# Splitting the first two weight tiles of a convolved projection, and multiplying half of the first, inside the projection before it

## The reference, cut to what matters

```python
h = rmsnorm(x, norm_g[l, 0]) * (1.0 + sc1) + sh1
z = h @ mix_in
za = dwconv3(z[..., :IN_COLS_A], mix_conv)
r, k, v, u = jnp.split(za, 4, -1)
qb, kb, vb = (t.reshape(B_, S_, N_HEADS_B, HEAD_DIM) for t in jnp.split(z[..., IN_COLS_A:], 3, -1))
```

## Time and profile before

| | us |
|---|---|
| median of 3 runs | 2668.36 |
| lowest and highest run | 2662.7 and 2673.42 |
| the profiled execution, its own time | 2661.84 |
| its span, first to last instruction | 2659.8 |
| TensorE busy in the span | 2489.5 (94%) |
| VectorE, ScalarE, GpSimd busy | 1674.4, 1158.0, 1063.9 |
| mean granted TensorE clock | 0.973 |

### The profile page before, as it was taken

One profiled execution on the slowest core, in us unless ns is written; L12 is line 12 of the kernel. 1 busy time (PEld: TensorE's weight loads), 2 busy tenths in 40 slices (PEclk: granted clock), 3 DMA queues, 4 the chain that ended last, 5 costly groups with the idle time before them and its releaser, 6 DMA issues. The chain is left out here.

```text
span 2659.8 us, 51660 instructions
## 1 busy us (share of the span) xinstructions
PE 2489.5 (94%) x21215; PEld 2005.1 (75%) x21215; DVE 1674.4 (63%) x2450; ACT 1158.0 (44%) x1886; POOL 1063.9 (40%) x717
## 2 busy tenths in 40 slices
PE   6998999798999989899999999987989999999998
PEld 5776666577888877778888878765777888887876
DVE  7775632474666546666565676856566666667686
ACT  5211343564555533444444444454444444444453
POOL 0301122202222202258888843331325787884333
PEclk9999999898999999999999999997999999999999
DMA  7776544803222124224343355231222434335423
GB/s 248 238 263 221 176 153 189 243 18 81 75 75 75 51 90 135 90 73 127 115 127 103 119 202 159 66 119 72 88 95 68 127 115 127 103 119 205 155 72 127
DMA packets 301965, 339.45 MB, mean 128 GB/s; under 512 B 29056, under 2 KB 207989, under 8 KB 301733
## 3 DMA queue, kind: packets, MB, share of 16 engines
q1 hardware_dynamic: 292092, 329.83, 38.4%
q10 hardware_dynamic: 9640, 6.33, 0.8%
HBM read 253.23 MB, written 82.88 MB: 126 GB/s over the span
## 5 line engine op out<-in xcount | busy, mean ns | idle before, releaser
L3410 POOL TENSOR_TENSOR first_over_u_lo<-first_over_u_raw,first_over_u_hi 128x512 fp32r<-128x512 f32 x210 | 319.5, 1529 | 120.2 <-ACT first_over_u_hi L3237 120.2
L3237 ACT ACTIVATE first_over_u_hi<-first_over_u_raw 128x512 fp32r<-128x512 f32 x210 | 128.6, 630 | 378.3 <-POOL first_over_u_raw L3428 147.5
L136 PE MATMUL cg_ps<-m_hi,first_over_u_hi 128*128 128x512 f32 x544 | 211.6, 389 | 0.0
L137 PE MATMUL cg_ps<-m_lo,first_over_u_hi 128*128 128x512 f32 x544 | 211.6, 389 | 0.0
L138 PE MATMUL cg_ps<-m_hi,first_over_u_lo 128*128 128x512 f32 x544 | 211.6, 389 | 0.0
L3486 DVE SCALAR_TENSOR_TENSOR cg_z<-cg_ps,top_conv_f,cg_z 128x1023 f32<-128x1023 f32 x84 | 107.8, 1283 | 73.9 <-ACT cg_z L3262 73.9
L136 PE MATMUL first_over_ps<-over_y_tx,first_over_u_hi 128*128 128x512 f32 x320 | 124.5, 389 | 0.0
L137 PE MATMUL first_over_ps<-over_y_tx,first_over_u_hi 128*128 128x512 f32 x320 | 124.5, 389 | 0.0
L138 PE MATMUL first_over_ps<-over_y_tx,first_over_u_lo 128*128 128x512 f32 x320 | 124.5, 389 | 0.0
L3410 POOL TENSOR_TENSOR first_over_u_lo<-cg_u_s,first_over_u_hi 128x512 fp32r<-128x512 f32 x80 | 103.4, 1292 | 50.5 <-ACT first_over_u_hi L3237 50.5
L138 PEld LDWEIGHTS cg_ps<-m_hi,first_over_u_lo 128*128 128x128 f32 x544 | 102.1, 188 | 21.4
(11 more groups left out here) (553 smaller groups left out, 7186.1 us busy)
## 6 DMA issues: line engine op xcount, KB each, us to landing
first_over_u_raw<-in_ffn_up SPq DMA_DIRECT2D x88, 512.0 KB, 5.0
qkv_mw<-in_ada_w SPq DMA_DIRECT2D x12, 2048.0 KB
scr_act<-cg_z SPq DMA_DIRECT2D x44, 512.0 KB, 2.6
raw_over_h_b<-in_ffn_down SPq DMA_DIRECT2D x56, 256.0 KB, 3.0
first_over_u_raw<-scr_act SPq DMA_DIRECT2D x44, 256.0 KB, 4.5
first_over_u_raw<-scr_asum SPq DMA_DIRECT2D x44, 256.0 KB, 2.6
scr_asum<-cg_over_split_sums SPq DMA_DIRECT2D x42, 256.0 KB
qkv_mw<-in_ada_w SPq DMA_DIRECT2D x8, 1024.0 KB, 11.5
```

The costliest lines, as they stand in the source:

```text
L136: nc.tensor.matmul(out, a_hi, b_hi, start=first, stop=False)
L137: nc.tensor.matmul(out, a_hi, b_lo, start=False, stop=False)
L3237: A(u_hi[:, n % RING], source(g, i), ACT.Copy).then_inc(uhi_done, 1)
L3410: G.tensor_tensor(u_lo[:, n % RING], source(g, i), u_hi[:, n % RING].bitcast(F32), ALU.subtract).then_inc(ulo_done, 1)
```

## The change

A class `FirstTiles` holds the raw, high and low parts of the first two weight tiles and the PSUM tile of the convolved projection, at addresses that are valid in both functions (its `ps` lies on the banks of `qkv_ps`; the high and low parts lie on the half of `qkv_w_hi` that column block 1 used). The splits of tiles 0 and 1 by ScalarE move into steps 20 and 21 of the q, k, v projection, after the copies that ScalarE makes there, and the two subtractions by GpSimd follow them. TensorE makes tile 0's product over the first 512 tokens in the function before: four of the eight k ahead of the last `add_up` (chunk 11), four behind it. The convolved projection then starts with `second_half(0)`.

```diff
--- before.py
+++ after.py
@@ -143,7 +143,29 @@
     t for f in range(WA // P) for t in (f, 2 * (WA // P) + f)]
 
 
-def features_and_qkv(nc, x_src, cond, mix_in, columns, x, xt, h_hi, h_lo, consts, rope_cos, rope_sin, qk_d, v_d, ada_w, ada_b, mod_d):
+class FirstTiles:
+
+    def __init__(self, nc, s, h_hi, h_lo):
+        self.nc, self.h_hi, self.h_lo = nc, h_hi, h_lo
+        self.raw = s.sb("raw", [P, 2, KT, P])
+        s.sb("x", [P, WA // P, S])
+        self.hi, self.lo = s.sb("w_hi", [P, 2, KT, P], F32R), s.sb("w_lo", [P, 2, KT, P], F32R)
+        self.ps = s.ps("ps", [P, 2, S])
+        self.hi_done, self.lo_done = s.sem("hi_done"), s.sem("lo_done")
+
+    def split(self, act, j):
+        self.nc.scalar.activation(self.hi[:, j], self.raw[:, j], ACT.Copy).then_inc(self.hi_done, 1)
+
+    def low(self, pool, j):
+        pool.wait_ge(self.hi_done, j + 1)
+        self.nc.gpsimd.tensor_tensor(self.lo[:, j], self.raw[:, j], self.hi[:, j].bitcast(F32), ALU.subtract).then_inc(self.lo_done, 1)
+
+    def products(self, k):
+        split_products(self.nc, self.ps[:, 0, 0:HALF], self.hi[:, 0, k, :], self.lo[:, 0, k, :], self.h_hi[:, k, 0:HALF], self.h_lo[:, k, 0:HALF],
+                       k == 0, k == KT - 1)
+
+
+def features_and_qkv(nc, x_src, cond, mix_in, columns, x, xt, h_hi, h_lo, consts, rope_cos, rope_sin, qk_d, v_d, ada_w, ada_b, mod_d, tiles):
 
 
 
@@ -156,8 +178,7 @@
     with ExitStack() as ctx:
         s = Scope(nc, ctx, "qkv")
         R = 4
-        with ExitStack() as octx:
-            w_next = Scope(nc, octx, "next").sb("w", [P, 2, KT, P])
+        w_next = tiles.raw
         w_raw = s.sb("w_raw", [P, R, WA])
         w_hi = s.sb("w_hi", [P, 2, KT, WA], F32R)
         w_lo = s.sb("w_lo", [P, 2, KT, WA], F32R)
@@ -341,6 +362,10 @@
                     for c in range(CM):
                         if summed_at(c) == cb * TT + t:
                             chunk_out(c)
+                    if cb == NC - 1 and t in (4, 5):
+                        act.wait_ge(next_loaded, 32)
+                        act.wait_ge(mm_done, TT * cb)
+                        tiles.split(act, t - 4)
                 if cb + 2 < NC:
                     split(cb + 2)
             for j in range(2):
@@ -360,6 +385,8 @@
                 pool.wait_ge(hi_done, n + 1)
                 nc.gpsimd.tensor_tensor(w_lo[:, cb % 2, k, :], w_raw[:, n % R, :], w_hi[:, cb % 2, k, :].bitcast(F32),
                                         ALU.subtract).then_inc(lo_done, 1)
+            tiles.low(pool, 0)
+            tiles.low(pool, 1)
 
         @block.vector
         def _(dve):
@@ -542,11 +569,17 @@
                         turn(n - 1)
                     for c in range(CM):
                         if summed_at(c) == n:
+                            if c == CM - 1:
+                                pe.wait_ge(tiles.lo_done, 1)
+                                pe.wait_ge(staged, n - 1)
+                                for k in range(KT // 2):
+                                    tiles.products(k)
                             pe.wait_ge(ms.acc_done, c + 1)
                             if c >= 2:
                                 pe.wait_ge(ms.row_done, c - 1)
                             ms.add_up(c % 2, c % 2)
-    return w_next
+            for k in range(KT // 2, KT):
+                tiles.products(k)
 
 
 CH = 64
...
@@ -580,8 +613,10 @@
     with ExitStack() as ctx:
         s = Scope(nc, ctx, "za")
         s.sb("w_place", [P, 2, KT, P])
-        w_hi, w_lo = s.sb("w_hi", [P, 2, KT, P], F32R), s.sb("w_lo", [P, 2, KT, P], F32R)
-        u, kt = s.sb("u", [P, KU, S]), s.sb("k", [P, KU, S])
+        u = s.sb("u", [P, KU, S])
+        s.sb("w_hi_place", [P, 2, KT, P]), s.sb("w_lo_place", [P, 2, KT, P])
+        w_raw, w_hi, w_lo, hi_done, lo_done = tiles.raw, tiles.hi, tiles.lo, tiles.hi_done, tiles.lo_done
+        kt = s.sb("k", [P, KU, S])
         rt, vt, both = (s.sb(n, [P, 2, S]) for n in ("r", "v", "both"))
         kk = u
         lw = s.sb("lw", [P, 3, KU, P])
@@ -590,14 +625,15 @@
         out = s.sb("out", [P, 4, S])
         pick, spread = s.sb("pick", [P, 32]), s.sb("spread", [P, P])
         rest, eps = s.sb("rest", [P, KU]), s.sb("eps", [P, 1])
-        ps, pr = s.ps("ps", [P, 2, S]), s.ps("pr", [P, 2, S])
+        s.ps("ps_place", [P, 2, S])
+        ps, pr = tiles.ps, s.ps("pr", [P, 2, S])
...
@@ -846,7 +882,8 @@
                 pe.wait_ge(bonus_in, f + 1)
                 product(f"H{f}", heads[:, :], both[:, f % 2, :], result(f"H{f}"))
 
-            for p in range(3):
+            second_half(0)
+            for p in range(1, 3):
                 tile(p)
             chunk_sum(0)
             tile(3)
@@ -912,10 +949,8 @@
             A = nc.scalar.activation
 
             def split(p):
-                if p >= 2:
-                    act.wait_ge(raw_loaded[p % 2], 16 * (p // 2))
-                if p >= 2:
-                    act.wait_ge(mm_done, p - 1)
+                act.wait_ge(raw_loaded[p % 2], 16 * (p // 2))
+                act.wait_ge(mm_done, p - 1)
                 A(w_hi[:, p % 2], w_raw[:, p % 2], ACT.Copy).then_inc(hi_done, 1)
 
             def middle(p):
@@ -987,8 +1022,6 @@
                 act.dma_start(mod_d[1, (E0 + c) * CHUNK:(E0 + c + 1) * CHUNK].rearrange("(o n) -> o n", o=1),
                               in_slot(bon, c)[0:1, :]).then_inc(m_stored[c % 2], 16)
 
-            split(0)
-            split(1)
             for p in range(3):
                 step(p)
             chunk_out(0)
@@ -1072,7 +1105,7 @@
                 pool.wait_ge(rated, f + 1)
                 G.tensor_tensor(both[:, f % 2, :], both[:, f % 2, :], kt[:, f, :], ALU.mult).then_inc(rated_k, 1)
 
-            for p in range(11):
+            for p in range(2, 11):
                 low(p)
             sum_rates(0)
             low(11)
...
```

More of the change, by code:

```diff
@@ L560, in project_and_prepare @@
 def project_and_prepare(nc, mix_in, conv_cols, h_hi, h_lo, w1, a1, g1, w2, a2, g2, tab, consts, z_d, lw_d, aa_d, kk_d, bon_d, gate_d, vr_d,
-                        ada_w, ada_b, mod_d, w_raw, heads_in, qk_d, bias_table):
+                        ada_w, ada_b, mod_d, tiles, heads_in, qk_d, bias_table):
     vec, heads = consts["vec"], consts["heads"]
@@ L596, in project_and_prepare @@
         out_stored = [s.sem(f"out_stored{i}") for i in range(4)]
-        (hi_done, lo_done, mm_done, mid_done, left_done, conv_done, hidden_loaded, net_loaded, tab_loaded, small_mm, act_read, dve_read,
+        (mm_done, mid_done, left_done, conv_done, hidden_loaded, net_loaded, tab_loaded, small_mm, act_read, dve_read,
          eps_set, rest_set, kk_in, sq_done, root_in, root_done, asum, rated, rated_k, bonus_in, vr_done, k_stored, gate_stored, vr_stored,
          bon_stored, kk_stored) = (s.sem(n) for n in (
-             "hi_done", "lo_done", "mm_done", "mid_done", "left_done", "conv_done", "hidden_loaded", "net_loaded", "tab_loaded", "small_mm",
+             "mm_done", "mid_done", "left_done", "conv_done", "hidden_loaded", "net_loaded", "tab_loaded", "small_mm",
              "act_read", "dve_read", "eps_set", "rest_set", "kk_in", "sq_done", "root_in", "root_done", "asum", "rated", "rated_k",
@@ L4241, in build @@
             h_hi, h_lo = hs.sb("hi", [P, KT, S], F32R), hs.sb("lo", [P, KT, S], F32R)
-            w_next = features_and_qkv(nc, x0, a["c"], a["mix_in"], groups, x, xt, h_hi, h_lo, consts, tab["rope_cos"],
-                             tab["rope_sin"], scr["qk"], scr["v"], a["ada_w"], a["ada_b"], scr["mod"])
+            with ExitStack() as octx:
+                tiles = FirstTiles(nc, Scope(nc, octx, "first_tiles"), h_hi, h_lo)
+            features_and_qkv(nc, x0, a["c"], a["mix_in"], groups, x, xt, h_hi, h_lo, consts, tab["rope_cos"],
+                             tab["rope_sin"], scr["qk"], scr["v"], a["ada_w"], a["ada_b"], scr["mod"], tiles)
             project_and_prepare(nc, a["mix_in"], consts["conv_a"], h_hi, h_lo, a["rwkv_w1"], a["rwkv_a1"], a["rwkv_g1"], a["rwkv_w2"],
                                 a["rwkv_a2"], a["rwkv_g2"], tab, consts, scr["z"], scr["lw"], scr["aa"], scr["kk"], scr["bon"],
-                                scr["gate"], scr["vr"], a["ada_w"], a["ada_b"], scr["mod"], w_next, heads_in, scr["qk"], tab["att_bias"])
+                                scr["gate"], scr["vr"], a["ada_w"], a["ada_b"], scr["mod"], tiles, heads_in, scr["qk"], tab["att_bias"])
         with ExitStack() as actx:
```

## The result

The changed kernel takes 2673.34 us in the median of 20 runs, the kernel before 2666.10 us in the median of 20: ratio 1.0026, 95% interval 1.0018 to 1.0035. That is 7.2 us slower by the medians (4.8 to 9.3 us by the interval), where +7 was forecast. (The kernel before was at 2668.36 when three runs of it were known; the later runs moved its median down by 2.3 us.) The profiled execution of the changed kernel took 2675.94 us, its span is 2674.0 us at a mean granted clock of 0.969.

A forecast was written before the change was run, and what follows sets the result against it. TensorE was taken to set the pace behind one hole, with tile 2's weights level with it. A barrier delay of 4.5 us plus 2.8 us of half clock, less a few tenths, gave +7: 2675.5 us, range 2663 to 2683.

The forecast's parts named there:

- Tile 2's weights take over: Convolved projection: TensorE, done early with tiles 0 and 1, waits some 12 us for tile 2's weights; chance 0.57.
- The subtractions delay the row sums by 2.0 us each: q, k, v projection, chunks 9 and 10: each GpSimd subtraction costs VectorE 2.0 us; bounds 0 and 2.7 us.
- The second twelve products: Behind the last sum, beside ScalarE's row copy and store: these products cost nothing or some tenths of a us.
- A few tenths come back: At tile 2: its subtraction may run beside a VectorE convolution rather than row sums, taking +7.3 to +7 us.
- The half clock: Behind the wait at tile 2: TensorE restarts at half clock, losing 2.8 us; bounds 0 and 3.2 us.
- Rival B: q, k, v projection: VectorE isn't delayed, or slack swallows its delay; +3.5 us, 2672 us; chance 0.22.
- Rival C: SyncE's list behind the barrier: tile 2's weights land sooner, making the kernel faster, 2658 to 2664 us; chance 0.11.
- Rival D: q, k, v projection: TensorE's clock also falls at the new waits, up to 2.8 us each, 2678 to 2681; chance 0.10.

The follow-up runs named there:

- splits only: Changed kernel without the early products; splits and subtractions of tiles 0 and 1 stay early, all of tile 0 multiplied in the next block: ratio 1.0012.
- subtractions on VectorE: Changed kernel with the two early subtractions on VectorE, between its chunks 10 and 11, instead of GpSimd: ratio 1.0005.
- all of it: Changed kernel, weights of tiles 2 and 3 loaded first, tile 0 convolved first, early subtractions on VectorE, nine not twelve products before the last sum: ratio 0.9964.
- idle products: Changed kernel with 46 products of 128x512, results unread, on TensorE between tile 1 and tile 2: ratio 1.0002.
- weights and convolution first: Changed kernel with weights of tiles 2 and 3 loaded first behind the barrier and tile 0 convolved before chunk 0's row sums: ratio 0.9978.
- weights first: Changed kernel with raw weights of tiles 2 and 3 at the head of SyncE's list behind the barrier: ratio 1.0002.

## Why the prediction was right

- **Tile 2's weights take over.** This held. The wait was forecast as some 12 us near 249 and is 11.43 us at 250.49, with 1.0 us of shift from ahead. The 11 us that TensorE gained at the block's start all came back there; with the weights and the convolution moved they stayed (0.9978).
- **The subtractions delay the row sums by 2.0 us each.** This held: 7.49 and 7.57 us. They put off the last sum as worked out: 217.25 - 190.27 = 26.98 us instead of 22.26, +4.7 where +4.5 was forecast. The kernel with the splits only has 2.0 of it alone; with the subtractions on VectorE 0.9 remains, where 0.7 was forecast for the twelve products. The two together cost more than 2.0 + 0.9, as either alone is partly taken up by the 1.93 us that TensorE waited there before, and both can't use the same wait.
- **The second twelve products "cost nothing or some tenths".** This is the step that failed, by 0.9 us. The first two rows below are VectorE's first work behind the barrier, in the kernel before and in the changed one; the last two are the last early product and the first one behind the barrier in the kernel with all of it.

```profile
215.87 0.17 DVE L1126 TENSOR_SCALAR za_rest<-top_vec 128x4 f32<-128x4 f32 x1 [4.42 <-PEq L58]
...
222.49 0.17 DVE L1159 TENSOR_SCALAR za_rest<-top_vec 128x4 f32<-128x4 f32 x1 [8.22 <-PEq L58]
...
216.44 0.39 PE L138 MATMUL first_tiles_ps<-h_hi,first_tiles_w_lo 128*128 128x512 f32 x1
218.09 0.47 PE L136 MATMUL first_tiles_ps<-h_hi,first_tiles_w_hi 128*128 128x512 f32 x1 [1.26 <-PEq L58]
```

  The sum of chunk 11 came 4.7 us later, but the first work behind the barrier 5.65 us later (32.22 us after chunk 8's sum instead of 26.57). In all six kernels with early products the first work behind the barrier starts 1.65 us after the last of them (220.84 to 222.49, 216.44 to 218.09). The distance from ScalarE's last store is not the same: 2.64 us in the kernel before (store at 213.23), 3.56 us in the changed one (218.93), 4.24 us in the one with all of it (213.85). So there the products set the barrier, no longer the store. The prediction held the end of the products (216) against the end of the barrier (215.85), and left out these 1.65 us between the two. The kernel with the subtractions on VectorE shows the same 0.9 us: +0.9 at its last sum, +1.8 at its barrier (28.40 us after chunk 8's sum).
- **"A few tenths come back".** It was 0.8 us: the list took 23.2 us instead of 23.7, and GpSimd's subtraction of tile 2 took 2.35 us instead of 2.69. The prediction had only the second of these, and the first isn't explained. These 0.8 us and the 0.9 us of the step before cancel, and that is luck: tile 2 is at +4.8, not +4.5.
- **The half clock.** It cost 2.5 us where 2.8 was forecast; the idle products gave 2.6 us back. That the medians give +7.2 against +7 is closer than their interval (4.8 to 9.3 us) can vouch for.
- **Rival B** (VectorE not delayed) is out by the same rows. **Rival C** had its place right, SyncE's list, and its condition wrong: nothing that was moved had held the list up. It had no second obstacle in it; there was one, tile 0's convolution behind chunk 0. **Rival D** isn't in the changed kernel's profile, but in two others with the same first block: in part of the executions it adds something, which the medians hold already.

## What to carry to other kernels

Before work is moved out of a hole, look for the wait behind the hole: here it was 0.59 us long, and its chain (a fixed list of loads that starts at the barrier) had nothing to do with the moved work, so it took back all that the hole gave. Once that chain was shortened, the next one showed, VectorE's own order; both had to be moved before the first move paid. And work put on an idle engine isn't free: here it slowed a busy one, on which a sum and a barrier hang, by more than that engine would have needed for the work itself.

## What the runs showed of the hardware

- A GpSimd subtraction of 128x1024 beside VectorE's row sums takes 2.0 to 2.1 us from VectorE (7.49 to 7.62 us for seven, 5.48 alone) and is itself stretched, from 2.35 us to 2.71 and 2.39 us in the changed kernel. The same subtraction on VectorE takes 1.18 us, so VectorE loses more by giving it away here than by doing it. The Trainium skill (SBUF — State Buffer, "Who interferes with whom") calls the ports that the two engines share an exclusive lock; that the other engine is blocked for the whole instruction it spells out for VectorE's two-port modes. For the two-input sums of this kernel the loss measured is somewhat less than the 2.4 to 2.7 us of the instruction.
- TensorE's clock fell at a pause of 2.56 us in one profile (weights and convolution first) and at one of 1.90 us in another (weights first), and not at those of 2.37 and 1.87 us in the changed kernel's or of 2.05 and 1.89 us in the idle products', whose code is the same there. So a pause of about 2 us costs in some executions and not in others; what decides it stays open.
- A wait of TensorE can cost more than its length: behind waits of 11.43, 11.01 and 4.99 us at tile 2 the first products were 0.43 us apart, and from there to the attention 2.5, 2.2 and 2.0 us more went by than in the kernel before; behind the 3.35 us of the splits only, the 0.19 us of the idle products and the 1.02 us at tile 3 of the weights and convolution first they ran at full clock.
